# A convolution's channel mean and mean of squares: four tiles added on GpSimd, then one matmul with ones

## The reference, cut to what matters

```python
def _layernorm(x, g, b):
    xf = x.astype(jnp.float32)
    mu = jnp.mean(xf, axis=-1, keepdims=True)
    var = jnp.mean(jnp.square(xf - mu), axis=-1, keepdims=True)
    ...
    u = cv * jax.nn.sigmoid(cg)
    full = jnp.concatenate([conv_state.astype(u.dtype), u], axis=1)
    c = lax.conv_general_dilated(full, conv_dw_w[:, None, :], (1,), 'VALID', ...)   # 31 taps, per channel
    c = jax.nn.silu(_layernorm(c + conv_dw_b, conv_ln_g, conv_ln_b))
    y_a = c @ w_conv_out
```

## Time and profile before

| | |
|---|---|
| median of 3 runs | 833.04 us (831.78 to 835.78) |
| span of the profiled execution | 831.2 us |
| TensorE busy, share of the span | 792.4 us, 95% |
| VectorE busy | 248.1 us, 30% |
| ScalarE busy | 154.2 us, 19% |
| GpSimd busy | 113.9 us, 14% |
| mean traffic of DMA | 322 GB/s over the span |

### The profile page before, as it was taken

How to read it: one execution, slowest core, us unless ns; L and a number is a source line. 1 busy time by engine, 2 the same in 40 slices (tenths; PEclk the granted TensorE clock), 3 DMA queues, 4 the chain that set the end, 5 groups by cost and what they waited for, 6 DMA issues and landing times.

```text
span 831.2 us, 9597 instructions
## 1 busy us (share of the span) xinstructions
PE 792.4 (95%) x3941; PEld 455.7 (55%) x3941; DVE 248.1 (30%) x528; ACT 154.2 (19%) x242; POOL 113.9 (14%) x135
## 2 busy tenths in 40 slices
PE   6999999999999999999999999999989989999996
PEld 4888888888888888873333333333323322333332
DVE  2159957486652212361011100111011011101102
ACT  3012422434312500140111111110100110010012
POOL 5100051265620000001110000001200000000001
PEclk9999999999999999999999999999999999999998
DMA  8824646669689682389999999999999999999992
GB/s 305 250 102 153 227 159 199 181 175 211 192 272 409 256 303 102 111 307 416 387 398 427 427 426 425 429 424 430 424 429 427 426 428 427 427 425 421 422 420 115
DMA packets 74388, 267.99 MB, mean 322 GB/s; under 512 B 5598, under 2 KB 37450, under 8 KB 58335
## 3 DMA queue, kind: packets, MB, share of 16 engines
q1 hardware_dynamic: 72666, 264.36, 82.1%
q0 software_dynamic: 528, 1.90, 0.6%
q10 hardware_dynamic: 1149, 1.09, 0.4%
HBM read 259.26 MB, written 8.55 MB: 322 GB/s over the span
## 4 chain that ended last, share of the span: by engine, by line
PE 82%; DMA 12%; DVE 2%; POOL 1%; ACT 1%; issue 0%; DVEq 0%; SPq 0%; POOLq 0%
PE bank L1507 24%; PE bank L1871 22%; PE bank L1909 11%; DMA slots<-in_w_expert_gate_dram 8%; PE bank L1767 7%; PE bank L1918 6%; DMA slot<-in_w_expert_gate_dram 4%; PE bank L1714 2%; PE bank L1550 2%; PE bank L1898 1%; DVE early L1374 1%; ACT wrep L931 1%; PE bank L1835 1%; PE bank L1597 1%; PE bank L1471 1%; PE bank L1782 1%
## 5 line engine op out<-in xcount | busy, mean ns | idle before, releaser
L1507 PE MATMUL bank<-hT,slots 128*128 128x264 f32 x896 | 207.3, 390 | 0.0
L1871 PE MATMUL bank<-slots,hT 128*64 128x512 f32 x680 | 188.9, 605 | 5.9 <-DMA slots<-in_w_expert_gate_dram 5.9
L1507 PEld LDWEIGHTS bank<-hT,slots 128*128 128x128 f32 x896 | 169.8, 192 | 29.0 <-issue 0.6
L1374 DVE TENSOR_TENSOR early<-early,bank 128x512 f32<-128x512 f32 x16 | 11.0, 688 | 386.0 <-PE bank L1871 386.0
L1871 PEld LDWEIGHTS bank<-slots,hT 128*64 128x64 f32 x680 | 57.9, 139 | 109.7 <-issue 99.4
L1909 PE MATMUL bank<-slots,wrep 128*64 128x512 f32 x336 | 103.5, 595 | 5.4 <-ACT wrep L931 5.4
L1871 PE MATMUL bank<-slot,hT 128*64 128x512 f32 x256 | 73.7, 594 | 2.3 <-DMA slot<-in_w_expert_gate_dram 2.3
L745 POOL COPY hT<-early 128x512 f32 x30 | 17.6, 614 | 371.1 <-PE bank L1871 286.1
L1918 PE MATMUL bank<-hT,diag 128*128 128x512 f32 x128 | 59.2, 605 | 0.2 <-ACT hT L943 0.2
L1909 PEld LDWEIGHTS bank<-slots,wrep 128*64 128x64 f32 x336 | 32.1, 137 | 49.7 <-issue 41.0
L1076 DVE SCALAR_TENSOR_TENSOR slot<-slot,rows_buf 128x256 f32<-128x256 f32 x120 | 48.1, 476 | 0.0
(11 more groups left out here) (290 smaller groups left out, 748.6 us busy)
## 6 DMA issues: line engine op xcount, KB each, us to landing
slots<-in_w_expert_gate_dram SPq DMA_DIRECT2D x18, 2048.0 KB, 28.1
slots<-in_w_expert_down_dram SPq DMA_DIRECT2D x18, 2048.0 KB, 28.8
slots<-in_w_expert_up_dram SPq DMA_DIRECT2D x16, 2048.0 KB, 29.7
slots<-in_w_in_dram SPq DMA_DIRECT2D x14, 2048.0 KB, 9.2
slot<-in_w_expert_gate_dram SPq DMA_DIRECT2D x8, 2048.0 KB, 25.1
slots<-in_w_expert_up_dram SPq DMA_DIRECT2D x9, 1024.0 KB, 29.4
slots<-in_w_expert_gate_dram SPq DMA_DIRECT2D x8, 1024.0 KB, 22.8
slot<-in_w_expert_up_dram SPq DMA_DIRECT2D x4, 2048.0 KB, 28.9
```

The source lines that it names most:

```text
L1374: dve.tensor_tensor(act.rearrange("s (f c) -> s f c", f=FT), act.rearrange("s (f c) -> s f c", f=FT), bank[UP][:, :].rearrange("s (c f) -> ...
L1507: last = mm(out, w[:, a, t * P:(t + 1) * P], hT[:, a, :], start=(a == 0), stop=(a == KT - 1))
L1871: last = mm(out[sl, :], xe[:, a, sl], expert_view(p, kind, e, a // 4)[:, a % 4, :], start=(a == 0), stop=(a == KT - 1))
```

## The change

`channel_sum` no longer takes the four tiles but one sum of them, made by GpSimd. GpSimd adds the first two tiles to the last two (128 x 528), waits for itself, and adds the two halves (128 x 264). TensorE then runs one matmul with ones instead of four. This is done for the convolution ("mean") and for its squares ("var"). The sum is kept in the first two tiles of `csq`.

TensorE's waits for the taps (`conv_ready`, `tap_done`) and for the squares (`ln_sq`) move to GpSimd, and TensorE waits for `sum_ready`. GpSimd's order, before 0, 1, 2, 3, s0, s1, ..., becomes 0, 1, sum of the convolution, 2, sum of the squares, 3, s0, s1, .... The pieces behind are in the same order as before.

```diff
+        csum = csq[:, 0:2, :]
...
-            for work in (0, 1, 2, 3, "s0", "s1", 4, "s2", "s3", 5, "s4", "s5", 6, "s6", "s7", 7, 8):
+            def tile_sum(n, src):
+                pool.tensor_tensor(csum, src[:, 0:2, :], src[:, 2:4, :], ALU.add).then_inc(halves_added, 1)
+                pool.wait_ge(halves_added, n + 1)
+                pool.tensor_tensor(csum[:, 0, :], csum[:, 0, :], csum[:, 1, :], ALU.add).then_inc(sum_ready, 1)
+
+            def conv_sum():
+                pool.wait_ge(conv_ready, 1)
+                pool.wait_ge(tap_done, CT * TAPS)
+                pool.wait_ge(misc.ready, misc.written("usrow"))
+                tile_sum(0, conv)
+
+            def square_sum():
+                pool.wait_ge(ln_sq, 1)
+                tile_sum(1, csq)
+
+            decayed_qk(0)
+            decayed_qk(1)
+            conv_sum()
+            decayed_qk(2)
+            square_sum()
+            decayed_qk(3)
+            for work in ("s0", "s1", 4, "s2", "s3", 5, "s4", "s5", 6, "s6", "s7", 7, 8):
...
-            def channel_sum(name, src):
+            def channel_sum(name, n):
+                pe.wait_ge(sum_ready, n)
                 proj.before_write(pe, name)
-                for c in range(CT):
-                    last = mm(bank[proj.bank(name)][:, 0:T], ones[:, 0:P], src[:, c, :], start=(c == 0), stop=(c == CT - 1))
-                last.then_inc(P_ready, 1)
+                mm(bank[proj.bank(name)][:, 0:T], ones[:, 0:P], csum[:, 0, :], start=True, stop=True).then_inc(P_ready, 1)
...
-            pe.wait_ge(conv_ready, 1)
-            pe.wait_ge(tap_done, CT * TAPS)
-            channel_sum("mean", conv)
+            channel_sum("mean", 1)
...
-            pe.wait_ge(ln_sq, 1)
-            channel_sum("var", csq)
+            channel_sum("var", 2)
```

More of the change, by code:

```diff
@@ L264, in hybrid_layer @@
             sem(n) for n in ("log_ready", "k_ready", "q_ready", "diff_ready", "decay_ready", "kq_ready"))
-        u_ready, prod_ready, tap_done, conv_ready, centred, ln_sq, ln_rstd, ln_scaled, conv_silu = (
-            sem(n) for n in ("u_ready", "prod_ready", "tap_done", "conv_ready", "centred", "ln_sq", "ln_rstd", "ln_scaled", "conv_silu"))
+        u_ready, halves_added, sum_ready, prod_ready, tap_done, conv_ready, centred, ln_sq, ln_rstd, ln_scaled, conv_silu = (
+            sem(n) for n in ("u_ready", "halves_added", "sum_ready", "prod_ready", "tap_done", "conv_ready", "centred", "ln_sq", "ln_rstd", "ln_scaled", "conv_silu"))
         state_in = [sem(f"state_in{i}") for i in range(2)]
```

## The result

The changed kernel took 831.97 us (median of 20 runs, 828.84 to 834.88), the kernel before 833.2 us in the runs beside it. The ratio is 0.9976 with a 95% interval of 0.9966 to 0.9985, that is 1.2 to 2.8 us less, where the forecast was 2.67 us less and 830.4 us. The two medians differ by 1.2 us and the means of the same runs (833.86 and 831.74) by 2.1, so the interval says more than any one of these differences. The profiled span is 828.4 us, within 0.1 us of the 828.5 forecast. That agreement is an accident, as will be seen: the front part gained less than forecast, and the expert stage of this one execution was shorter for another reason.

A forecast was written before the change was run, and what follows sets the result against it. TensorE was taken to bound the front part (95% busy), with the expert stage's DMA stream starting and refilled behind it. -2.67 us removed + 0 + 0 took 833.04 to 830.4 us, range 828.4 to 833.4.

The forecast's parts named there:

- What is removed: TensorE, both sites: six matmuls of 0.445 us leave its stream, 2.67 us, 1.33 us at each site.
- The first sum: GpSimd's sum for the mean: ready at 144.6 us (145.7 slow), TensorE there at 149.62, so no cost.
- The second sum: GpSimd's sum for var: ready at 155.4 us (156.5 slow), TensorE there at 158.1, 1.6 to 2.7 to spare.
- slowest rate: GpSimd's line 705, 3.9 ns a column: a sum takes 3.1 us instead of 2.0, kept for the bound.
- The moved pieces: GpSimd pieces 2 and 3 behind the sums: piece 2 ends about 149.4, piece 3 begins at 160.4; no cost.
- The check of the chain of sample values: Before line 1531: the chain hangs on TensorE and the values move by 2.6 of the 2.67 us.
- The first rival: Line 1531, 230 us: v_rows chain stays, wait grows 0.9 to 3.55 us, time 833.0, halfway 831.7; chance 0.11.
- The sum: Whole kernel: -2.67 + 0 + 0 us, with at most some 0.5 us lost; 830.4 us.
- The second rival: Expert stage: the weight stream sets the end whatever TensorE does before; time stays 833.0; chance 0.07.
- The third rival: TensorE before var: second sum late; gain lost at a 7.4 us sum, 0.5% slower at 11.5; chance 0.05.

The follow-up runs named there:

- both repairs: Changed kernel with level_diff(4) ahead of turned_values(4) and (5) on VectorE, and decayed_qk(7) ahead of the last two sample heads on GpSimd; ratio to before 0.9976.
- changed with the new order: Changed kernel with decayed_qk(7) ahead of sample_head(6) and (7) on GpSimd; ratio to before 0.9974.
- padded kernel: Changed kernel with 24 empty instructions in TensorE's stream ahead of the cross scores (the trace shows none of them); ratio to before 0.9968.
- VectorE with the new order: Against the kernel before: both sums added on VectorE, and decayed_qk(7) ahead of sample_head(6) and (7) on GpSimd; ratio 0.9971.
- late sum: Changed kernel with the first addition of the squares made four times instead of once, each behind the last; ratio to before 1.0086.
- sums on VectorE: Changed kernel with both sums added on VectorE instead of GpSimd, which keeps its old order; ratio to before 0.9982.
- changed again: The changed kernel once more, nothing altered, for the scatter of its profile; ratio to before 0.9986.

## Why the prediction was right, point by point

**What is removed: right.** Six matmuls of 0.445 us are 2.67 us, and the ruler shows 2.67 in each kernel in which nothing else interferes at the site, and 1.34 to 1.35 for one site.

**The first sum: right.** Forecast to be ready at 144.6, it ended at 144.75, with TensorE some 4.5 us away.

**The second sum: the step that failed.** The sum was to be ready at 155.4, at 156.5 if GpSimd ran at its slowest rate, and TensorE was to have 1.6 us or more to spare. It was ready at 158.15, and TensorE lost 11.58 - 11.07 = 0.5 us on the ruler against the kernels without that delay. The duration was 1.3 + 0.75 us as sized, but the bound was wrong. I took the slowest rate per column as the worst that VectorE can do to GpSimd, and had even read the earlier trace rows as mutual slowing, though by my own shift VectorE's subtractions were to begin at 155.3, right beside the addition that I had placed until 155.4. The delay measured here is not a rate times the columns; it lasted 2.84 and 2.85 us for quite different remainders, half a microsecond more than the other engine's work. The bound should have been the end of that work, 157.6, plus an addition.

**The moved pieces: right.** Piece 2 ended at 149.4 as forecast, piece 3 started at 160.78 (forecast 160.4, plus what `var` had lost).

**The check of the chain of sample values: right in its direction, short in its size.** The first transfers were issued at 159.00, where I had 158.6, and `var` itself was late. The last was issued 2.44 us earlier than before, so all links that were said to hang on TensorE moved in this profile. What I had not allowed for is that the landing itself varies. It took 16.0 to 16.2 us in the two profiles of before, and 17.4 to 17.5 in the two of the changed kernel, and anything from 15.8 to 17.6 over all fourteen. The first rival, that the gain is given back at 230 us, is thus true in part: the wait went from 0.4 and 0.9 us to 1.4 and 1.8. Why the landing took longer stays open. Kernels with the same issue times had 16.2 (both repairs) and 17.6 (changed with the new order), so it isn't the earlier issue alone.

The links don't hang on TensorE alone either. In the padded kernel, which has the changed kernel's sums, the last transfer is issued 56.7 us after t0, against 53.6 in the changed kernel and 55.9 before, and lands after 15.8 us. SyncE waited there for VectorE's `states_add`, eight instructions of which took 5.46 us, where the changed kernel needs 2.18. Six of them took 0.35 us each, and the two that began while GpSimd was in a product took 2.0 each; GpSimd's two products kept their 1.9 us. VectorE's timeline, POOL's, and SyncE's:

```profile
194.68 5.46 DVE L1115 SCALAR_TENSOR_TENSOR ga<-ga,rows_buf,slot 128x128 f32<-128x128 f32 x8
```
```profile
196.19 3.82 POOL L706 TENSOR_TENSOR slot<-slot,early 128x1024 f32<-128x1024 f32 x2 [3.15 <-DMA slot<-v_rows]
```
```profile
205.74 1.05 SPq L470 DMA_DIRECT2D slots<-v_rows  x1
```

Here VectorE bore the delay, and the chain of the first rival stayed where it was. VectorE with the new order shows the same 5.46 us; its order hides it. That the contention of the two engines moves this chain by 3 us is in no line of the forecast.

**The sum.** By the ruler, the front part gained 82.5 - 81.3 = 1.2 us up to the cross scores (mean of the two profiles of each kernel): 2.67 less 0.5 at `var` and 1.0 before the cross scores. The measured gain is 1.2 to 2.8 us. I forecast 2.67 with at most 0.5 lost; the sign and "within 0.5%" were right, and the full size lies inside the interval, near its upper end. How much of it usually arrives is not settled: two profiles a side give 1.2 us, the median spans give 2.55 (831.5 less 828.95) and 2.05 in the repetition, and the median span of before itself differed by 0.65 us from that of its own repetition. The profiled span agrees with the forecast only because the first profile of before had the drop of the clock after 370 us and that of the changed kernel had not, 1.5 us.

**The second rival, that the stream sets the end: falls.** The stage from the gather on is as long in all kernels, but for the 1.7 us of the clock, so what is gained or lost up to the gather goes to the end of the span.

**The third rival, slower by a late sum: its price was wrong.** I had TensorE's loss grow one for one with lateness, and 0.5% slower only with a sum of 11.5 us. In the late sum the sum took 9.1 us (152.61 to 161.71). By that price the loss is 9.1 - 7.4 = 1.7 us, and 2.0 were lost at the site; but the kernel was 0.66 to 1.06% slower, because the clock fell as well. A late sum was likelier to hurt than I made it.

## What to carry to other kernels

An instruction moved to GpSimd must be checked against what VectorE does at that moment, and not only against GpSimd's own durations. If two-input instructions of VectorE may overlap with it, count it as finished only after them. The same holds the other way: the sums on VectorE were held up once by a product of GpSimd (2.47 us instead of 0.43). Before moving work off a saturated engine, look also for what that engine waits on further down. A stream order that makes a piece wait for a transfer that it doesn't need was worth as much here as the whole change (0.9981 alone). And compare two profiles from a common instant close to the change: spans differed by 1.5 us between two executions of the same code.

## What the runs showed that I had not expected

- A GpSimd addition of 264 columns took 0.75 us alone and 3.59 us when its last 0.1 us overlapped with VectorE's two-input instructions. It ended 0.6 us after them in all four profiles in which it meets them so (changed, changed again, changed with the new order, padded). VectorE lost nothing there. In other places VectorE bore the delay: 2.47 us instead of 0.43 for the first sum's second addition, and 5.46 instead of 2.18 in `states_add`. There too GpSimd's instruction had begun before VectorE's (142.63 against 143.17, and 196.19 against 196.26), as it had in the changed kernel (154.55 against 155.19), where GpSimd lost. So who begins first doesn't decide it.
- A wait of TensorE can cost more than its length. After 4.4 us of idle time the granted clock was 0.50 for some 6.8 us (3.3 us lost), and in one profile of several, after 1.8 us, the cross scores took 3.68 instead of 2.05 us.
- The measured time less the span is 1.7 us in the four kernels that change no sum or one, and 2.7 to 2.8 us in the eight that change both (medians of 6 to 35 runs each). By the spans of its runs the changed kernel is at 828.95 us (median of 20), and the kernel before at 831.5 (median of 35 runs beside other kernels); this 1 us takes a part of that gain back in the times. What happens in that microsecond no profile shows, and the one run that was to find it was inconclusive. It stays open.
